# A hybrid encoder trunk on one core: the mask added on POOL, and P transposed with diag(1/sum)

## The reference, cut to what matters

```python
def attend_block(qb, qib, wib, qp, qc, ks, vs, kis, k_pos, k_chunk, rel_table, n_sel):
    ...
    _, idx = lax.top_k(score, n_sel)
    ok = jnp.take_along_axis(adm, idx, axis=1)
    ...
    logits = jnp.einsum('qgrd,qkgd->qgrk', qg, kg).astype(jnp.float32) * HEAD_DIM ** -0.5
    bias = rel_table[rel_bucket(k_pos[idx] - qp[:, None])]
    logits = logits + bias.reshape(nq, n_sel, N_KV_HEADS, GROUP).transpose(0, 2, 3, 1)
    logits = jnp.where(ok[:, None, None, :], logits, NEG_INF)
    p = jax.nn.softmax(logits, axis=-1).astype(vg.dtype)
    return jnp.einsum('qgrk,qkgd->qgrd', p, vg).reshape(nq, N_HEADS * HEAD_DIM)
```

## Time and profile before

| | |
|---|---|
| time, median of 3 runs | 1787.86 us |
| profiled execution | 1787.89 us, span 1786.1 us |
| mean granted TensorE clock | 0.999 of full speed |
| TensorE busy | 1769.6 us (99%), 10034 records |
| VectorE busy | 1066.6 us (60%) |
| ScalarE busy | 716.3 us (40%) |
| POOL busy | 212.9 us (12%) |

### The profile page before, as it was taken

How to read it: one execution, slowest core, us unless ns; L and a number is a source line. 1 busy time by engine, 2 the same in 40 slices (tenths; PEclk the granted TensorE clock), 3 DMA queues, 4 the chain that set the end, 5 groups by cost and what they waited for, 6 DMA issues and landing times.

```text
span 1786.1 us, 27858 instructions
## 1 busy us (share of the span) xinstructions
PE 1769.6 (99%) x10034; PEld 1733.9 (97%) x10034; DVE 1066.6 (60%) x1856; ACT 716.3 (40%) x1139; POOL 212.9 (12%) x258
## 2 busy tenths in 40 slices
PE   9999999999999999999999999999999999999998
PEld 8988999999999999999999999999999889999998
DVE  7876855544487755554476655554457867555533
ACT  5365433333378433333232333333323664333331
POOL 5000300001115400001100200000140004000011
PEclk9999999999999999999999999999999999999999
DMA  8311333333333433334433333333455113433441
GB/s 304 125 36 60 119 120 126 118 119 129 119 117 106 135 129 117 120 115 141 130 118 129 119 118 117 117 119 128 136 171 180 60 48 102 133 129 118 130 138 62
DMA packets 63844, 216.96 MB, mean 121 GB/s; under 512 B 7153, under 2 KB 8769, under 8 KB 63521
## 3 DMA queue, kind: packets, MB, share of 16 engines
q1 hardware_dynamic: 59520, 202.25, 34.3%
q0 software_dynamic: 3280, 12.12, 2.3%
q10 hardware_dynamic: 976, 1.70, 0.3%
HBM read 212.38 MB, written 3.66 MB: 121 GB/s over the span
## 4 chain that ended last, share of the span: by engine, by line
PE 92%; DVE 4%; ACT 3%; issue 1%; DMA 0%; DVEq 0%; ACTq 0%
PE bank L703 27%; PE bank L702 27%; PE bank L701 27%; PE bank L901 1%; PE bank L878 1%; PE bank L857 1%; PE bank L859 1%; PE bank L858 1%; DVE w_lo L1310 1%; PE bank L920 1%; ACT w_hi L1028 1%; PE bank L884 1%; PE bank L927 0%; PE bank L804 0%; PE bank L928 0%
## 5 line engine op out<-in xcount | busy, mean ns | idle before, releaser
L701 PE MATMUL bank<-a_hi,w_hi 128*128 128x400 f32 (+2 forms) x1936 | 673.4, 348 | 1.6 <-DVE w_lo L1310 1.1
L1310 DVE TENSOR_TENSOR w_lo<-raw,w_hi 128x1024 fp32r<-128x1024 f32 x382 | 490.3, 1288 | 306.7 <-ACT w_hi L1028 305.1
L702 PE MATMUL bank<-a_lo,w_hi 128*128 128x400 f32 (+2 forms) x1936 | 666.0, 344 | 0.0
L703 PE MATMUL bank<-a_hi,w_lo 128*128 128x400 f32 (+2 forms) x1936 | 665.3, 344 | 0.0
L1028 ACT ACTIVATE w_hi<-raw 128x1024 fp32r<-128x1024 f32 x382 | 399.9, 1052 | 345.6 <-PE bank L703 338.0
L701 PEld LDWEIGHTS bank<-a_hi,w_hi 128*128 128x128 f32 (+1 forms) x1936 | 362.5, 187 | 6.0 <-issue 1.9
L703 PEld LDWEIGHTS bank<-a_hi,w_lo 128*128 128x128 f32 (+1 forms) x1936 | 364.9, 188 | 0.7
L702 PEld LDWEIGHTS bank<-a_lo,w_hi 128*128 128x128 f32 (+1 forms) x1936 | 362.7, 187 | 2.6
L703 PE MATMUL bank<-h_hi,w_lo 128*128 128x400 f32 (+1 forms) x704 | 240.8, 342 | 0.0
L702 PE MATMUL bank<-h_lo,w_hi 128*128 128x400 f32 (+1 forms) x704 | 240.1, 341 | 0.0
L701 PE MATMUL bank<-h_hi,w_hi 128*128 128x400 f32 (+1 forms) x704 | 239.2, 340 | 0.0
(11 more groups left out here) (255 smaller groups left out, 1754.4 us busy)
## 6 DMA issues: line engine op xcount, KB each, us to landing
raw<-in_w_all SPq DMA_DIRECT2D x382, 512.0 KB, 3.4
bias_p<-rel_scratch POOLq DMA_DIRECT2D x2, 2176.0 KB, 10.6
k_s<-in_ck_t POOLq DMA_DIRECT2D x4, 512.0 KB, 8.5
v_c<-in_cv POOLq DMA_DIRECT2D x2, 1024.0 KB, 15.5
ki_s<-in_cki_t POOLq DMA_DIRECT2D x4, 256.0 KB, 5.5
x<-in_x_t SPq DMA_DIRECT2D x2, 400.0 KB, 6.3
x<-in_x_t ACTq DMA_DIRECT2D x2, 400.0 KB, 6.8
out_v_t<-v_f POOLq DMA_DIRECT2D x2, 400.0 KB, 5.1
```

What stands on the lines that cost most here:

```text
L701: pe.matmul(out, wh, hi[:, kc, c0:T], start=(first and n == 0), stop=False)
L702: pe.matmul(out, wh, lo[:, kc, c0:T], start=False, stop=False)
L703: mm = pe.matmul(out, wl, hi[:, kc, c0:T], start=False, stop=(last and n == len(blocks) - 1))
L1310: nc.vector.tensor_tensor(w_lo[:, s, :], raw[:, s, :], w_hi[:, s, :].bitcast(F32), ALU.subtract).then_inc(lo_ready, 1)
```

## The change

It has three parts.

1. *Mask and bias of prompt items.* TensorE's mask matmul (L877) goes. POOL makes the sum of bias (read backwards) and mask for each prompt item in one of three buffers `bm`, and VectorE's `reduced` reads that in place of the bias. Sample and meta items stay as they are.
2. *Transposes.* VectorE's `normalise` becomes `inverse`: only the reciprocal. POOL multiplies the identity with it into one of four tiles `diag`, and `turn` becomes a plain f32 matmul of `lg` with `diag` in place of the transpose. The exponentials stay unscaled in `lg`.
3. *Last remainder.* At VectorE's last step of the core `low` of the last group comes before `half_out`, not behind it.

`bm` and `diag` lie in the buffers of `sq`, `sqsum` and `std`, free in the core, and one new buffer. On POOL all new work, `rows_of_core`, stands behind the outputs of v and ahead of the squares.

```diff
@@ gpsimd @@
+            def rows_of_core(a):
+                pool.wait_ge(in_bias, 96 * (a + 1))
+                pool.wait_ge(vt_done, a + 1)
+                def biased(j):
+                    _, gp, (t, gi, r) = ITEMS[a][PROMPT[a][j]]
+                    keys = width(ITEMS[a][PROMPT[a][j]])
+                    pool.wait_ge(masks, 3 * a + 1 + t)
+                    if j >= 3:
+                        pool.wait_ge(lg_ready, IB[a] + PROMPT[a][j - 3] + 1)
+                    pool.tensor_tensor(bm[j % 3][:, 0:keys], backwards(bias_p[:, 4 * (2 * gp + gi) + r, 0:keys]), mask[t][:, 0:keys],
+                                       ALU.add).then_inc(biased_ready, 1)
+                j = 0
+                for n in range(N_IT[a]):
+                    while j < len(PROMPT[a]) and PROMPT[a][j] <= n + 2:
+                        biased(j)
+                        j += 1
+                    pool.wait_ge(rinv_ready, IB[a] + n + 1)
+                    if n >= 4:
+                        pool.wait_ge(tr_done, UB[a] + USE[a][n - 4][0] + 1)
+                    pool.tensor_scalar(diag[n % 4][:], ident, rinv[:, n % 8:n % 8 + 1], None, ALU.mult).then_inc(diag_ready, 1)
...
                     pool.dma_start(v_t[a], v_f[:]).then_inc(out_sem, 16)
+                    rows_of_core(a)
@@ tensor, logits @@
-                        pe.wait_ge(masks, 3 * a + 1 + t)
                         pe.wait_ge(evacuated, t0 + 9 + 4 * gp + r + 1)
-                        pe.matmul(ps, ident_b[:], mask[t][:, 0:keys], start=True, stop=False)
-                        mm = pe.matmul(ps, q_t[:, 4 * gp + r, 128 * t:128 * t + 128], kz[:, gi, gp, 0:keys], start=False, stop=True)
+                        mm = pe.matmul(ps, q_t[:, 4 * gp + r, 128 * t:128 * t + 128], kz[:, gi, gp, 0:keys], start=True, stop=True)
@@ tensor, turn @@
-                    pe.wait_ge(pn_ready, IB[a] + n + 1)
+                    pe.wait_ge(diag_ready, IB[a] + n + 1)
                     for i, (c, _) in enumerate(turned(ITEMS[a][n])):
                         col = 256 * h + 128 * i
-                        mm = pe.transpose(bank[4 + k % 2][:, col:col + 128], lg[n % NL][:, c:c + 128], ident)
+                        mm = pe.matmul(bank[4 + k % 2][:, col:col + 128], lg[n % NL][:, c:c + 128], diag[n % 4][:],
+                                       start=True, stop=True)
@@ vector, reduced @@
-                        bias = bias_p[:, 4 * (2 * gp + gi) + r, 0:keys]
+                        j = PROMPT[a].index(n)
+                        dve.wait_ge(biased_ready, PB[a] + j + 1)
+                        bias = bm[j % 3][:, 0:keys]
@@ vector, normalise @@
-                def normalise(n):
-                    keys = width(ITEMS[a][n])
+                def inverse(n):
                     dve.wait_ge(ex_done, IB[a] + n + 1)
-                    b8 = n % 8
-                    chain(nc.vector.reciprocal(rinv[:, b8:b8 + 1], esum[:, b8:b8 + 1]))
-                    nc.vector.tensor_scalar(lg[n % NL][:, 0:keys], lg[n % NL][:, 0:keys], rinv[:, b8:b8 + 1], None,
-                                            ALU.mult).then_inc(pn_ready, 1)
+                    nc.vector.reciprocal(rinv[:, n % 8:n % 8 + 1], esum[:, n % 8:n % 8 + 1]).then_inc(rinv_ready, 1)
@@ vector, the loop @@
-                        normalise(n - LAG_NORM)
+                        inverse(n - LAG_NORM)
+                    if n == N_IT[a] + LAG_LO - 1:
+                        low(len(LAST[a]) - 1)
...
-                        if e + LAG_LO == n and OUT[a][g][1]:
+                        if e + LAG_LO == n < N_IT[a] + LAG_LO - 1 and OUT[a][g][1]:
                             low(g)
```

More of the change, by code:

```diff
@@ L130 @@
 GB = [0, len(GROUPS[0])]
+PROMPT = [[n for n, it in enumerate(ITEMS[a]) if it[0] == "prompt"] for a in range(2)]
+PB = [0, len(PROMPT[0])]
 def buffer_of(a, g):
@@ L244, in program @@
         gate_s, up_s, silu_s, hid_s = (sb(n, [128, T]) for n in ("gate_s", "up_s", "silu_s", "hid_s"))
+        rsq = cursor[0]
         sq, sqsum, std, rstd = (sb(n, [128, T]) for n in ("sq", "sqsum", "std", "rstd"))
@@ L271, in program @@
         ident = cst[:, C_ID:C_ID + 128]
+        bm = [at("bm0", [128, NP_TOK], F32, rsq), at("bm1", [128, NP_TOK], F32, rsq + 1088), sb("bm2", [128, NP_TOK])]
+        diag = [at(f"diag{n}", [128, 128], F32, rsq + 2176 + 512 * n) for n in range(4)]
         R = Region(rh, hbytes)
@@ L379, in program @@
         lg_done, lg_ready = sem("lg_done"), sem("lg_ready")
-        ex_done, pn_ready = sem("ex_done"), sem("pn_ready")
+        ex_done, diag_ready = sem("ex_done"), sem("diag_ready")
+        rinv_ready, biased_ready = sem("rinv_ready"), sem("biased_ready")
         tr_done = sem("tr_done")
@@ L1559, in reduced @@
                         t, gi, r = what
-                        bias = bias_p[:, 4 * (2 * gp + gi) + r, 0:keys]
+                        j = PROMPT[a].index(n)
+                        dve.wait_ge(biased_ready, PB[a] + j + 1)
+                        bias = bm[j % 3][:, 0:keys]
                     elif kind == "sample":
-                        bias = bias_s[:, gp, :]
+                        bias = backwards(bias_s[:, gp, :])
                     else:
-                        bias = bias_m[:, gp, :]
-                    nc.vector.tensor_tensor_reduce(lg[n % NL][:, 0:keys], logit_bank(a, n)[:, 0:keys], backwards(bias), -1.0, 3.0e38,
+                        bias = backwards(bias_m[:, gp, :])
+                    nc.vector.tensor_tensor_reduce(lg[n % NL][:, 0:keys], logit_bank(a, n)[:, 0:keys], bias, -1.0, 3.0e38,
                                                    ALU.add, ALU.min, nmx[:, n % 8:n % 8 + 1]).then_inc(lg_ready, 1)
-                def normalise(n):
-                    keys = width(ITEMS[a][n])
+                def inverse(n):
                     dve.wait_ge(ex_done, IB[a] + n + 1)
-                    b8 = n % 8
-                    chain(nc.vector.reciprocal(rinv[:, b8:b8 + 1], esum[:, b8:b8 + 1]))
-                    nc.vector.tensor_scalar(lg[n % NL][:, 0:keys], lg[n % NL][:, 0:keys], rinv[:, b8:b8 + 1], None,
-                                            ALU.mult).then_inc(pn_ready, 1)
+                    nc.vector.reciprocal(rinv[:, n % 8:n % 8 + 1], esum[:, n % 8:n % 8 + 1]).then_inc(rinv_ready, 1)
                 def low(g):
```

## The result

The changed kernel takes **1804.53 us** (median of 4 runs, 1804.47 to 1804.58) against 1787.88 us for the kernel before on the same chip: a ratio of 1.0091, interval 1.0075 to 1.0107. It is slower by 16.7 us. The forecast was 1804.6 us.

What follows compares the result with a forecast made beforehand. TensorE, busy 99% of the span, was taken to bound the kernel. 1787.9 + 25.8 (transposes) - 5.5 (mask) - 0.8 (first items) - 2.8 (last remainder) = 1804.6 us, +0.9%; range 1800.8 to 1809.5 us, held at 0.78.

Steps and rivals of the forecast that it cites:

- Transposes: In the cores of layers 0 and 3, 226 transposes become plain f32 matmuls, each 0.114 us more on TensorE: +25.8 us.
- The lower bound of +24.6: Low end for the 226 transposes turned into plain matmuls in the cores, taking 0.22 us a call: +24.6 us.
- Mask passes: In both cores, 32 narrow and 32 wide mask matmuls leave TensorE: -5.5 us (-5.2 to -5.9).
- The f32 load: L878's weight load behind L920 groups, at 8 prompt items: if another 0.09 us showed in each, 0.7 us lost.
- First items: First four items of each core: VectorE, late there, loses normalising products, but POOL may delay splits: -0.8 us (-3.0 to +3.0).
- the added waits: In the cores, VectorE waits for POOL's sum, with one step of slack, and TensorE for its diagonal, with more.
- The last remainder: End of each core: remainder made before the last addition to x, so TensorE's next tile needn't wait: -2.8 us.
- POOL: POOL's new core work, 1.3 to 1.7 us per wide item against TensorE's 2.0 us step: keeps up, costed at nothing.
- The first rival: POOL bounds the core's wide items if a sum costs 1.6 us or more; 1821 us at 2.1; chance 0.08.
- The second and third rivals: Core turns: second, plain matmul costs what a transpose does, 1778.8 us (0.04); third, four times as much, 1853 us (0.02).
- The fourth: Rival, chance 0.08: in the cores, VectorE held up, late diagonals or f32 loads eat the gains; 1811 to 1814 us.
- the end of the normalising product on VectorE: In both cores some 30 us leave VectorE, which waits for TensorE: gain costed at nothing, except in the first four items.

Runs made afterwards that it cites:

- the plain matmuls alone: The kernel before with only its 226 transposes of P replaced by plain f32 matmuls with the same identity, nothing moved to POOL: 1811.91 us, ratio 1.0133.

## Why the prediction was right

**Transposes.** Predicted +25.8 us, measured +25.7 by starts. The step that carried it was to look for another line of the same trace with the same operand form and count its records, L927 and L928. The Trainium skill (TensorE: Matmul & The Clock Gate, Terms, xbus) gives a factor of four for the transpose mode in f32. It was rightly left: the plain matmuls alone show a factor of two. The lower bound of +24.6 does not follow from the numbers beside it: 226 x (0.220 - 0.109) is 25.1. The experiments with this part alone and with it undone, +24.0 and -24.8, agree, each with a microsecond of other waits in it.

**Mask passes.** Predicted -5.5, measured -5.9. The f32 load that was to show behind a group of L920 doesn't: the start behind such a group comes after 0.31 us in both kernels.

**First items.** Predicted -0.8 (-3.0 to +3.0), measured +0.2. The step that failed is in the added waits: "POOL has more than one step (2.0 us) for 0.3 us of work". The second and third step of a core have no turn and no values and are 0.8 to 0.9 us long, not 2.0; the diagonal costs 0.60, not 0.3; and the split beside it, which I had priced only as a loss to VectorE, cost POOL 1.1 us. Here VectorE's split had its 1.2 us and POOL was shut out; which of two is shut out I had not asked. The kernel before could have told me, and I misread it. This row of POOL stands right ahead of those of the earlier trace rows:

```profile
1483.70 1.18 POOL L573 TENSOR_TENSOR sq<-x 128x400 f32<-128x400 f32 x1 [1.24 <-DVE x L1353]
```

The split of 1484.16 came while this instruction ran (to 1484.88), and that delayed it; the sum of 1484.95, which I had blamed, came while the split ran (to 1485.96) and was itself held up, 1.91 us against a mean of 1.29.

**The last remainder.** Predicted -2.8, measured -2.8, alone and with the rest.

**POOL.** Its sum took 0.70 us for 272 columns where I had 0.9 to 1.3, its diagonal 0.60 where I had 0.3: 1.3 together for a wide item, and POOL idles between wide items of the changed kernel. The first rival did not come. Its threshold, a mean step of 2.0 us, was not right: the run with the sums made twice lost time already in narrow items, at 1.55 us against steps of 1.24. In the changed kernel a narrow item costs POOL about 1.0 us, so it is there, and not in the wide items, that least is to spare. The second and third rivals fell with the 452 records. The fourth came true in one place, the first diagonal (1.1 us in each core), and the waits that went gave it back.

**What the sum hid.** I put the end of the normalising product on VectorE at nothing, because VectorE waits for TensorE. That is so where the second part stands alone. With sums on POOL it is wrong: they shut the product out, and the first part alone costs 6.5 us where I had it at a gain of 5.5. The gain of the mask is there in the changed kernel only because the product is gone. The three parts taken alone give +6.5, +24.9 and -2.9, 28.5 us, against 16.7 together. A forecast of the first part by the same steps would have missed its sign. My forecast was right for the whole and had no reason in it why the first part needs the second. Its mechanism for the large term was right; that the whole came out within 0.1 us was luck, since terms off by up to 1.0 us cancelled, and since the first part never stood without the second.

So the change gives TensorE 25.7 us of passes to be rid of 98 products on an engine that was waiting. Most of what VectorE loses beside POOL's sums is had back for one wait on POOL, with the product left where it was.

## What to carry to other kernels

Before an operation is replaced on the bounding engine, find a line of the same trace with the new operand form and count records per call; here that one row gave the largest term to 0.1 us. Work moved to POOL is priced by what VectorE does in the same moment: two instructions that one event releases on both engines meet again and again (56 of 64 sums here), and a wait that puts one behind the other can be worth more than its own delay. An engine's work for an item is set against the shortest steps in the kernel, not against their mean. Parts of a change that share an engine are to be forecast singly too, since a sum can be right while a part has the wrong sign.

## What the runs showed of the hardware

A product with one input in SBUF (`tensor_scalar`, f32) on VectorE went from 0.30 to as much as 0.83 us beside a POOL sum; a POOL `tensor_scalar` went from 0.60 to between 1.49 and 1.69 beside a VectorE instruction with two inputs in SBUF (the split; 13 diagonals of the changed kernel). A VectorE reduction with one input in PSUM kept its 0.31 and 0.44 us beside POOL's work. The Trainium skill (SBUF — State Buffer, Who interferes with whom) has `tensor_scalar` among those that can take the shared ports, and calls the one that starts second fully blocked; the traces agree in size, 0.83 being about 0.12 more than a whole sum of 0.71. They don't show the order. The product was the one shut out in all 56 meetings of the kernel with the mask on POOL alone (the sum kept its 0.46 or 0.71), yet in 55 of them its recorded start is the earlier one, by some 0.03 us. So which of the two is shut out can be read from the durations, and not from recorded starts that close together.

POOL's diagonal of 128 columns takes 0.60 us, nearly as much as its 424-column `tensor_scalar` elsewhere (745 ns on the mean). Its sums grow with the columns, 0.46 for 144 and 0.70 for 272. Why the diagonal doesn't was not tried.
